# The ring of weight slots, with each slot a tensor of its own, 32 bytes further apart than a multiple of 2048

## The chip, the cores and the metric

The kernel runs on one core of one Trainium2 chip. The metric is the time of one execution on the device in microseconds (us). Lower is better. Weights, inputs and the output lie in HBM; everything else stays in SBUF and PSUM.

## What is computed

Two transformer-like blocks over 512 tokens of width 1024, one after the other. What matters here is that both are mostly matrix products of a 512-token activation with weights that are read once from HBM. The activations are kept transposed, features on the partitions.

```python
# first block, two layers
h = h + fourier_na_mixer(hn, w_in_ab, rpb, w_out_ab)        # layer 0: 1024 -> 2048, 1024 -> 1024
h = h + short_gated_conv_mixer(hn, w_in_c, conv_c, w_out_c) # layer 1: 1024 -> 3072, 1024 -> 1024
h = h + memory_cross_attention(norm(h), m, wq, wkv, wo)     # both; wkv acts on 256 memory rows
h = h + conv_ffn(norm(h), w_up, conv_w, conv_b, w_down)     # both: 1024 -> 4096, 2048 -> 1024
# second block, one layer
proj = u @ w_in                                             # 1024 -> 9232, cut into 12 parts
h = h + merged(retention(proj), gated_delta(proj)) @ w_o
h = h + (silu(a) * b) @ w_down,  a, b = conv(norm(h) @ w_up)  # 1024 -> 5632, 2816 -> 1024
return rmsnorm(h)
```

All of it is float32 in the reference.

## The kernel before

Every large product is cut into weight units of 256 rows by 512 columns. There are 379 of them (`n_units`), numbered u in the order in which they are used by the list `phases`. A unit passes through one of five slots of a ring (`RING = 5`, slot `u % RING`), and in that slot through four hands:

1. SP's queue loads it into `w_raw` (line 410; two transfers of half the width for the feed-forward "up" products). Before it issues, it waits until TensorE has used the unit that had the slot before: `w_used` at least `u - RING + 1`.
2. ScalarE (ACT) copies `w_raw` to `w_hi` in the rounded type fp32r (line 523, `split`), when the load has landed.
3. GpSimd (POOL) subtracts, `w_lo = w_raw - w_hi` (line 486, `lo`). `w_lo` lies on `w_raw`, byte for byte.
4. TensorE (PE) waits for `lo_done` and makes 24 products per unit (line 929, `products`): for each of four blocks of 128 columns and each of the two 128-row halves, three of them, which are hi by hi, hi by the low part of the activation, and lo by hi. The activation is split into high and low parts in the same way (`XH`, `XL`, or the slots of `HID`). Mostly the weights are the stationary operand (128x128) and 512 tokens stream. In the phases by token, and in the second half of each `kv` phase, the activation is stationary and 512 weight columns stream. `kv` (lines 1070 and 1073) has 256 memory rows: eight units of 24 products with 256 columns, then eight units of 12 products with 512 columns, in each of the two layers.

So there are 363 units of 24 products and 16 of 12, together 8,904 products with a ring operand. The other matmuls (attention, retention, delta rule, statistics) are plain float32 and read tiles that are not in the ring.

ACT, DVE and POOL run their own streams in program order, tied by semaphores. ACT's copies of weight units are put between its other work by `split_to`, up to four units (`LEAD`) ahead of the product that it evacuates.

Where things lie in a partition follows from the order of allocation; each tensor starts on a multiple of 32 bytes. `H`, `XH`, `XL` take 16,384 bytes each and start at 1,152. The ring follows: `w_raw` with `w_lo` on it (5 x 4,096 bytes) at 50,304, and `w_hi` (5 x 4,096) at 70,784. So every slot of both, and `XH` and `XL`, start at the same place modulo 2048. Then come `R`, `LNT`, `RC`, `LNC`, `ACC`, `SQ`, `par`, `cst`, `eps_c`, `sm`, and the arena that holds `HID` and all the tiles placed with `at(...)`. Its origin `a0` is pushed up until it equals `w_hi_at` modulo 512; it is 104,064, with 352 bytes skipped, and that is 512 bytes past the ring's place modulo 2048.

Of the kernel before, what the change touches and what calls it, by code (L numbers as in the profile page):

```python
# [18 lines left out]
F32 = mybir.dt.float32  # L19
F32R = mybir.dt.float32r  # L20
# [4 lines left out]
P = 128  # L25
# [6 lines left out]
UC = 512  # L32
# [54 lines left out]
def program(nc, ins, out):  # L87
    ctx = ExitStack()
    with ctx:
        def sb(name, shape, dt=F32):  # L90
            return ctx.enter_context(nc.sbuf_tensor(name, shape, dt))
# [5 lines left out]
        H = sb("H", [P, KT, T])  # L97
        XH = sb("XH", [P, KT, T], F32R)
        XL = sb("XL", [P, KT, T], F32R)
        w_raw = sb("w_raw", [P, RING, 2, UC])  # L100
        w_lo = nc.alloc_sbuf_tensor_at("w_lo", [P, RING, 2, UC], F32R, offset=nc.sbuf_base - RING * 2 * UC * 4)
        w_hi_at = nc.sbuf_base
        w_hi = sb("w_hi", [P, RING, 2, UC], F32R)
        R = sb("R", [P, T])
        LNT = sb("LNT", [P, T])
        RC = sb("RC", [P, NCH])
# [294 lines left out]
        @block.sync  # L401
        def _(sp):
            def load(mat, k, c_of, slot, freed):

                for s, v in freed:
                    sp.wait_ge(s, v)
                view = mat.rearrange("(k p) n -> p k n", p=P)
                at_col = 0
                for c, width in c_of:
                    sp.dma_start(w_raw[:, slot, :, at_col:at_col + width],  # L410
                                 view[:, 2 * k:2 * k + 2, c:c + width]
                                 ).then_inc(w_loaded[slot], 16)
                    at_col += width

            xv = ins["xT"].rearrange("(k p) t -> p k t", p=P)
            sp.dma_start(par[:, :], ins["params"]).then_inc(c_loaded, 16)
            for name, mat, nk, groups in phases:
                u0, per = first[name], nk // 2
                if name == "rqk":
                    sp.wait_ge(h_upd, KT * (rp_index["wo1"] + 1))  # L420
                    for tab, src in ((COS, "rot_cos"), (SIN, "rot_sin"), (AGE, "age")):
                        sp.dma_start(tab[:, :], ins[src]).then_inc(t_loaded, 16)
                if name == "dab":

                    u = u0
                    sp.wait_ge(w_used, u - RING + 1)
                    view = mat.rearrange("(k p) n -> p k n", p=P)
                    dst = w_raw[:, u % RING, :, :].rearrange("p a (b c) -> p (a b) c", c=P)
                    at_col = 0
                    for c, width in groups[0]:  # L430
                        sp.dma_start(dst[:, :, at_col:at_col + width], view[:, :, c:c + width]
                                     ).then_inc(w_loaded[u % RING], 16)
                        at_col += width
                    sp.wait_ge(rg_dve, 6)
                    sp.dma_start(LVM[:, :, :], ins["levels"]).then_inc(l_loaded, 16)
                    continue
                if name == "rv":

                    sp.wait_ge(bn_dve, 4 + KT)
                    sp.dma_start(h_dram, H[:, :, :].rearrange("p k t -> p (k t)")).then_inc(h_saved, 16)  # L440
                for g in range(len(groups)):
                    if name == "wo2" and g == 1:
                        sp.wait_ge(dn_dve, 4)
                        sp.wait_ge(h_saved, 16)
                        sp.dma_start(H[:, :, :].rearrange("p k t -> p (k t)"), h_dram).then_inc(h_back, 16)
                    for k in range(per):
                        u = u0 + g * per + k
                        freed = [(w_used, u - RING + 1)] if u >= RING else []
                        load(mat, k, groups[g], u % RING, freed)
                        if name == "out0" and (g, k) == (0, per - 1):  # L450

                            sp.wait_ge(f1_done, NA_H)
                            mv = ins["memT"].rearrange("(k p) t -> p k t", p=P)
                            sp.dma_start(M[:, :, :], mv).then_inc(m_loaded, 16)
                        if u < KT // 2:

                            sp.dma_start(H[:, 2 * u:2 * u + 2, :], xv[:, 2 * u:2 * u + 2, :]).then_inc(x_loaded[u], 16)
                        if u == 0:
                            sp.dma_start(cst[:, :, :], ins["consts"]).then_inc(c_loaded, 16)
                    if name == "in0" and g == 1:  # L460

                        sp.dma_start(FC[:, :, :], ins["fourier_seq"]).then_inc(f_loaded, 16)
                        sp.dma_start(GC[:, :], ins["fourier_grp"]).then_inc(f_loaded, 16)
                        rp = ins["rpb"]
                        for h in range(NA_H):
                            for i in range(2):
                                src = bass.AP(rp.tensor, (h * 15 + i) * RPB_PW, [[1, GRID_W], [RPB_PW, NA_ROWS], [1, GRID_W]])
                                sp.dma_start(B2[GRID_W * i:GRID_W * (i + 1), h, :, :], src).then_inc(b_loaded, 16)

            ov = out.rearrange("(k p) t -> p k t", p=P)  # L470
            for k in range(KT):
                sp.wait_ge(fin_dve, k + 1)
                sp.dma_start(ov[:, k, :], H[:, k, :]).then_inc(out_stored, 16)
            sp.wait_ge(out_stored, 16 * KT)


        @block.gpsimd
        def _(pool):
            nc.gpsimd.memset(eps_c[:, 0:1], EPS)
            nc.gpsimd.memset(eps_c[:, 1:2], GN_EPS).then_inc(pad_zero, 1)  # L480

            def lo(u):

                s = u % RING
                pool.wait_ge(hi_done, u + 1)
                nc.gpsimd.tensor_tensor(w_lo[:, s, :, :], w_raw[:, s, :, :], w_hi[:, s, :, :].bitcast(F32),  # L486
                                        ALU.subtract).then_inc(lo_done, 1)

            early = first["out0"]
            for u in range(early):  # L490
                lo(u)

            pool.wait_ge(b_loaded, 16 * 2 * NA_H)
            n = 0
            for i in range(2):
                half = B2[GRID_W * i:GRID_W * (i + 1), :, :, :].rearrange("p h s c -> p (h s) c")
                lowc = half[:, :, 0:GRID_W - NA_KW]
                nc.gpsimd.affine_select(out=lowc, in_=lowc, compare_op=ALU.is_ge, fill=-1e30,
                                        base=NA_KW // 2 - (GRID_W - 1),
                                        pattern=[[0, NA_H * NA_ROWS], [1, GRID_W - NA_KW]],  # L500
                                        channel_multiplier=1).then_inc(b2_sel, 1)
                n += 1
                pool.wait_ge(b2_sel, n)
                high = half[:, :, NA_KW:GRID_W]
                nc.gpsimd.affine_select(out=high, in_=high, compare_op=ALU.is_ge, fill=-1e30,
                                        base=NA_KW // 2 - 1 - NA_KW + GRID_W - 1,
                                        pattern=[[0, NA_H * NA_ROWS], [-1, GRID_W - NA_KW]],
                                        channel_multiplier=-1).then_inc(b2_sel, 1)
                n += 1
                pool.wait_ge(b2_sel, n)  # L510
            for u in range(early, n_units):
                lo(u)
# [3 lines left out]
        def _(act):  # L516
            state = {"split": 0}

            def split(u):

                s = u % RING
                act.wait_ge(w_loaded[s], load_value[u])
                nc.scalar.activation(w_hi[:, s, :, :], w_raw[:, s, :, :], ACT.Copy).then_inc(hi_done, 1)  # L523

            def split_to(end):

# [387 lines left out]
        def _(pe):  # L914
            def products(u, k, bank, x_hi_t, x_lo_t, tokens_out, start, stop):
# [3 lines left out]
                for m in range(4):  # L919
                    for j in range(2):  # L920
                        kt = 2 * k + j
                        for n in range(3):
                            wt = w_lo[:, slot, j, :] if n == 2 else w_hi[:, slot, j, :]
                            xt = x_lo_t[:, kt, :] if n == 1 else x_hi_t[:, kt, :]
                            if tokens_out:
                                a, b = xt[:, m * P:(m + 1) * P], wt
# [120 lines left out]
            def kv(l):  # L1047
# [4 lines left out]
                for g in range(4):  # L1052
# [5 lines left out]
                    for k in range(4):  # L1058
# [3 lines left out]
                        for m in range(4 if g < 2 else 2):  # L1062
                            for j in range(2):
                                kt = 2 * k + j
                                for n in range(3):
                                    wt = w_lo[:, s, j, :] if n == 2 else w_hi[:, s, j, :]
                                    xt = ML[:, kt, :] if n == 1 else MH[:, kt, :]
                                    begin, end = kt == 0 and n == 0, kt == KT - 1 and n == 2
                                    if g < 2:
# [291 lines left out]
            def block2():  # L1361
# [12 lines left out]
                u = first["dab"]  # L1374
                pe.wait_ge(lo_done, u + 1)
                pe.wait_ge(rb_dve, 1)
                hi = w_hi[:, u % RING, :, :].rearrange("p a (b c) -> p (a b) c", c=P)
                lo = w_lo[:, u % RING, :, :].rearrange("p a (b c) -> p (a b) c", c=P)
                for kt in range(KT):
                    for n, (a, b) in enumerate(((hi, XH), (hi, XL), (lo, XH))):  # L1380
                        mm = nc.tensor.matmul(ps[:, 0, :], a[:, kt, :], b[:, kt, :], start=kt == 0 and n == 0,
# [715 lines left out]
```

## Time and profile before

| what | value |
|---|---|
| median of 3 runs | 2449.18 us (2447.05 to 2452.76) |
| the profiled execution's own time | 2449.59 us |
| its span, first to last instruction | 2447.8 us |
| PE busy | 2354.3 us, 96% |
| PE weight loads busy | 1922.7 us, 79% |
| DVE, ACT, POOL busy | 999.8, 864.0, 972.0 us |
| DMA | 218.23 MB, mean 89 GB/s |
| granted TensorE clock, mean | 0.990 of 2.4 GHz |

The span leaves out 1.8 us of the execution's own time. A busy PE is not a PE at its peak: the pace of the products is read from how many fit into a stretch without a gap.

### The profile page before, as it was taken

To read this page: it belongs to the slowest core of one execution; us is meant where nothing else is said; L and a number is where in the kernel's file an instruction comes from. 1 tells how busy PE (TensorE), PEld (TensorE's weight loads), DVE (VectorE), ACT (ScalarE), POOL (GpSimd) and SP (SyncE) were. 2 spreads that over 40 slices of the span, in tenths; PEclk is the share of its full clock that TensorE was granted. 3 is DMA by queue.
4 is the path that set the end of the run, shared out by engine and by line. 5 is a ranking of instruction groups with operands and counts; after the bars stand their busy time and mean duration, and the time that the engine had idled before them with its cause. 6 is when DMAs were issued, how large, how long until landed. Compare 5 with 4: busy or idle time off the path is not lost.

```text
span 2447.8 us, 25636 instructions
## 1 busy us (share of the span) xinstructions
PE 2354.3 (96%) x10910; PEld 1922.7 (79%) x10910; DVE 999.8 (41%) x1222; ACT 864.0 (35%) x1044; POOL 972.0 (40%) x389
## 2 busy tenths in 40 slices
PE   8989999999999999999999999988998999999997
PEld 6748878888887887888887668867877888888885
DVE  4253034342143212444237231567368333666601
ACT  4245344233322433432344462351352243322221
POOL 4506524544444642444435224330140144455441
PEclk9999999999999999999999999999999999999998
DMA  6204313333333531333333213420230033333331
GB/s 186 95 17 140 118 44 95 101 98 95 95 95 94 154 96 53 97 101 95 108 111 108 65 44 106 112 65 18 55 84 18 27 95 129 96 102 95 95 96 68
DMA packets 148562, 218.23 MB, mean 89 GB/s; under 512 B 18641, under 2 KB 75217, under 8 KB 148193
## 3 DMA queue, kind: packets, MB, share of 16 engines
q1 hardware_dynamic: 147328, 212.38, 28.9%
q10 hardware_dynamic: 1120, 4.23, 0.5%
q8 instruction: 86, 1.41, 0.2%
q14 instruction: 28, 0.22, 0.0%
HBM read 212.34 MB, written 4.23 MB: 88 GB/s over the span
## 4 chain that ended last, share of the span: by engine, by line
PE 91%; DVE 5%; ACT 2%; issue 1%; DMA 0%; POOL 0%; SPq 0%; DVEq 0%; ACTq 0%
PE ps L929 76%; PE ps L1070 2%; PE ps L1073 2%; PE ps L1291 1%; PE ps L1086 1%; PE ps L1109 1%; DVE MT L1858 1%; PE ps L1280 1%; PE ps L1179 1%; PE ps L1192 1%; PE ps L1016 1%; PE ps L1232 1%; DVE MM L1862 0%; PE ps L952 0%; PE ps L1308 0%
## 5 line engine op out<-in xcount | busy, mean ns | idle before, releaser
L486 POOL TENSOR_TENSOR w_lo<-w_raw,w_hi 128x1024 fp32r<-128x1024 f32 x379 | 960.4, 2545 | 1435.6 <-ACT w_hi L523 1435.4
L929 PE MATMUL ps<-XH,w_hi 128*128 128x512 f32 x1792 | 703.2, 392 | 12.7 <-DVE XL L1419 11.8
L523 ACT ACTIVATE w_hi<-w_raw 128x1024 fp32r<-128x1024 f32 x379 | 395.4, 1056 | 874.0 <-DMA w_raw<-ffn_w_up 123.9
L929 PE MATMUL ps<-XH,w_lo 128*128 128x512 f32 x1792 | 698.3, 390 | 0.0
L929 PE MATMUL ps<-XL,w_hi 128*128 128x512 f32 x1792 | 698.1, 390 | 0.0
L929 PE MATMUL ps<-HID,w_hi 128*128 128x512 f32 x1760 | 542.9, 390 | 4.1 <-DVE TY L1641 2.4
L929 PEld LDWEIGHTS ps<-XH,w_hi 128*128 128x128 f32 x1792 | 337.0, 188 | 85.5 <-issue 14.2
L929 PEld LDWEIGHTS ps<-XL,w_hi 128*128 128x128 f32 x1792 | 337.1, 188 | 71.7 <-issue 2.4
L929 PEld LDWEIGHTS ps<-XH,w_lo 128*128 128x128 f32 x1792 | 336.9, 188 | 70.6
L929 PEld LDWEIGHTS ps<-HID,w_hi 128*128 128x128 f32 x1760 | 330.1, 188 | 74.9 <-issue 3.4
L929 PE MATMUL ps<-HID,w_lo 128*128 128x512 f32 x880 | 342.4, 389 | 0.0
L929 PEld LDWEIGHTS ps<-HID,w_lo 128*128 128x128 f32 x880 | 165.2, 188 | 34.5
L1429 DVE TENSOR_TENSOR H<-ps,H 128x512 f32<-128x512 f32 x64 | 42.3, 683 | 365.0 <-PE ps L929 365.0
L1578 DVE TENSOR_TENSOR GP<-ps,R 128x1024 f32<-128x1024 f32 x16 | 19.6, 1224 | 177.5 <-PE ps L929 177.5
L1280 PE MATMUL ps<-MM,AT 128*128 128x128 f32 x384 | 58.9, 302 | 26.5 <-DVE MM L1862 12.0
L1280 PEld LDWEIGHTS ps<-MM,AT 128*128 128x128 f32 x384 | 50.7, 207 | 34.2 <-DVE MM L1862 18.1
L1529 DVE TENSOR_TENSOR QX<-ps,R 128x2048 f32<-128x2048 f32 x4 | 9.2, 2292 | 157.6 <-PE ps L929 157.6
L1916 DVE SCALAR_TENSOR_TENSOR CV<-GP,par,CV 128x512 f32<-128x512 f32 x88 | 69.9, 863 | 0.0
L533 ACT ACTIVATE SQ<-H 128x512 f32<-128x512 f32 x63 | 39.7, 630 | 64.9 <-DVE H L1429 33.0
L1908 DVE TENSOR_TENSOR GP<-ps,R 128x2048 f32<-128x2048 f32 x11 | 25.2, 2291 | 76.2 <-PE ps L929 76.2
L1291 PE MATMUL ps<-MT,T 128*128 128x128 f32 x384 | 54.9, 285 | 0.5
L1405 DVE TENSOR_TENSOR ACC<-ACC,SQ 128x512 f32<-128x512 f32 x63 | 50.2, 797 | 6.5 <-ACT SQ L533 4.5
(318 smaller groups left out, 2307.0 us busy)
## 6 DMA issues: line engine op xcount, KB each, us to landing
w_raw<-w_in SPq DMA_DIRECT2D x72, 512.0 KB, 3.7
w_raw<-ffn_w_up SPq DMA_DIRECT2D x128, 256.0 KB, 2.9
w_raw<-w_up SPq DMA_DIRECT2D x88, 256.0 KB, 3.1
w_raw<-xa_wkv SPq DMA_DIRECT2D x32, 512.0 KB, 3.6
w_raw<-ffn_w_down SPq DMA_DIRECT2D x32, 512.0 KB, 3.7
w_raw<-w_in_c SPq DMA_DIRECT2D x24, 512.0 KB, 3.7
w_raw<-w_down SPq DMA_DIRECT2D x22, 512.0 KB, 3.6
w_raw<-w_in_ab SPq DMA_DIRECT2D x16, 512.0 KB, 4.1
```

The costliest lines, as they stand in the source:

```text
L486: nc.gpsimd.tensor_tensor(w_lo[:, s, :, :], w_raw[:, s, :, :], w_hi[:, s, :, :].bitcast(F32), ALU.subtract).then_inc(lo_done, 1)
L523: nc.scalar.activation(w_hi[:, s, :, :], w_raw[:, s, :, :], ACT.Copy).then_inc(hi_done, 1)
L533: nc.scalar.activation(ACC[:, :] if c == 0 else SQ[:, :], H[:, c, :], ACT.Square).then_inc(sq_done, 1)
L929: mm = nc.tensor.matmul(ps[:, bank + m, :], a, b, start=start and j == 0 and n == 0, stop=stop and j == 1 and n == 2)
L1070: mm = nc.tensor.matmul(ps[:, bank + m, 0:NMEM], wt[:, m * P:(m + 1) * P], xt, start=begin, stop=end)
L1073: mm = nc.tensor.matmul(ps[:, bank + m, :], xt[:, m * P:(m + 1) * P], wt, start=begin, stop=end)
L1280: mm = nc.tensor.matmul(ps[:, pb(p) + 2, cols_], AT[:, p, cols_], MM[:, p, cols_], start=True, stop=True)
L1291: mm = nc.tensor.matmul(ps[:, pb(p) + 3, cols_], T1[:, p, cols_], MT[:, hh, cols_], start=True, stop=True)
L1405: nc.vector.tensor_tensor(ACC[:, :], ACC[:, :], SQ[:, :], ALU.add).then_inc(acc_done, 1)
L1429: nc.vector.tensor_tensor(H[:, c, :], ps[:, (c + flip) % 8, :], H[:, c, :], ALU.add).then_inc(h_upd, 1)
L1908: nc.vector.tensor_tensor(GP4[:, :, 2:T + 2], banks(bank), over(R[:, :], 4), ALU.mult).then_inc(up2_dve, 1)
L1916: nc.vector.scalar_tensor_tensor(out=CV4[:, q, :], in0=GP4[:, q, i:T + i], scalar=of(w0 + 2 * nf * i, q), in1=CV4[:, q, :], op0=ALU.mult, ...
```

## The change

The three ring tensors become lists of five tensors each. Slot i now holds its `w_raw`/`w_lo` (4,096 bytes), directly behind it its `w_hi` (4,096 bytes), and behind that an unused tensor `gap` of 32 bytes. All uses index the list in place of the slot dimension; shapes, instructions, order and waits stay as they are.

```diff
-        w_raw = sb("w_raw", [P, RING, 2, UC])
-        w_lo = nc.alloc_sbuf_tensor_at("w_lo", [P, RING, 2, UC], F32R, offset=nc.sbuf_base - RING * 2 * UC * 4)
         w_hi_at = nc.sbuf_base
-        w_hi = sb("w_hi", [P, RING, 2, UC], F32R)
+        w_raw, w_lo, w_hi, gap = [], [], [], []
+        for i in range(RING):
+            w_raw.append(sb(f"w_raw{i}", [P, 2, UC]))
+            w_lo.append(nc.alloc_sbuf_tensor_at(f"w_lo{i}", [P, 2, UC], F32R, offset=nc.sbuf_base - 2 * UC * 4))
+            w_hi.append(sb(f"w_hi{i}", [P, 2, UC], F32R))
+            gap.append(sb(f"gap{i}", [P, 8]))
...
-                    sp.dma_start(w_raw[:, slot, :, at_col:at_col + width],
+                    sp.dma_start(w_raw[slot][:, :, at_col:at_col + width],
...
-                nc.gpsimd.tensor_tensor(w_lo[:, s, :, :], w_raw[:, s, :, :], w_hi[:, s, :, :].bitcast(F32),
+                nc.gpsimd.tensor_tensor(w_lo[s][:, :, :], w_raw[s][:, :, :], w_hi[s][:, :, :].bitcast(F32),
                                         ALU.subtract).then_inc(lo_done, 1)
...
-                nc.scalar.activation(w_hi[:, s, :, :], w_raw[:, s, :, :], ACT.Copy).then_inc(hi_done, 1)
+                nc.scalar.activation(w_hi[s][:, :, :], w_raw[s][:, :, :], ACT.Copy).then_inc(hi_done, 1)
...
-                            wt = w_lo[:, slot, j, :] if n == 2 else w_hi[:, slot, j, :]
+                            wt = w_lo[slot][:, j, :] if n == 2 else w_hi[slot][:, j, :]
```

The same replacement stands in the load of the `dab` unit (line 428), in `kv` (line 1066) and in the products of `dab` (lines 1377 and 1378).

## Rows read from the trace of the kernel before

**Rows 1.** The page's busy times of the engines.
```profile
span 2447.8 us, 25636 instructions
PE 2354.3 (96%) x10910; PEld 1922.7 (79%) x10910; DVE 999.8 (41%) x1222; ACT 864.0 (35%) x1044; POOL 972.0 (40%) x389
```

**Rows 2.** The page's chain that ended last, by engine.
```profile
PE 91%; DVE 5%; ACT 2%; issue 1%; DMA 0%; POOL 0%; SPq 0%; DVEq 0%; ACTq 0%
```

**Rows 3.** The chain in order of time: start us, us, what.
```profile
10.87 0.67 DVE XL L1419
11.55 0.25 issue
11.79 19.24 PE ps L929 x72
31.04 0.86 PE ps L952 x2
...
211.54 23.03 PE ps L1070 x192
234.57 21.79 PE ps L1073 x96
...
300.76 6.91 PE ps L1086 x32
...
394.70 261.14 PE ps L929 x1152
...
656.71 114.27 PE ps L929 x504
```

**Rows 4.** Windows: stretch, PE, PEld, DVE, ACT, POOL busy, clock, DMA share, GB/s.
```profile
211.50:234.60 23.10, 23.10 (x194) 23.10 (x193) 7.96 (x12) 13.09 (x16) 16.46 (x8) 1.00 0.61 181
234.60:256.40 21.80, 21.80 (x97) 18.02 (x96) 0.00 (x0) 10.31 (x10) 19.38 (x9) 1.00 0.64 190
400.00:650.00 250.00, 250.00 (x1104) 207.02 (x1103) 94.81 (x105) 78.55 (x88) 120.73 (x48) 1.00 0.32 97
```

**Rows 5.** One line's instructions: ns min/median/max, first and last start.
```profile
L486 POOL TENSOR_TENSOR w_lo<-w_raw,w_hi x379: 2342/2401/6995, 6.9 to 2406.1; 128x1024 fp32r<-128x1024 f32 x190
L523 ACT ACTIVATE w_hi<-w_raw x379: 1039/1060/1065, 5.8 to 2405.0; 128x1024 fp32r<-128x1024 f32 x190
L1587 DVE SCALAR_TENSOR_TENSOR CV<-GP,par,CV x64: 734/739/745, 405.9 to 1162.5; 128x512 f32<-128x512 f32 x64
```

**Rows 6.** DMA issues of the page: KB each, median us to landing.
```profile
w_raw<-w_in SPq DMA_DIRECT2D x72, 512.0 KB, 3.7
w_raw<-ffn_w_up SPq DMA_DIRECT2D x128, 256.0 KB, 2.9
```

**Rows 7.** Timeline of kv of the first layer, POOL and PEld.
```profile
219.98 18.98 POOL L486 TENSOR_TENSOR w_lo<-w_raw,w_hi 128x1024 fp32r<-128x1024 f32 x8 [6.64 <-ACT w_hi L523]
...
222.77 0.19 PEld L1070 LDWEIGHTS ps<-MH,w_hi 128*128 128x128 f32 x1
```

**Rows 8.** The chain after rotary: start us, us, what.
```profile
1312.79 1.07 ACT w_hi L523
1313.86 0.07 issue
1313.93 2.37 POOL w_lo L486
```

**Rows 9.** Who waited for whom: us in total, times, longest.
```profile
POOL w_lo L486 <- ACT w_hi L523: 1435.4, 285, 110.8
SPq L410 <- PE ps L929: 2054.0, 335, 116.6
```

More of the change, by code:

```diff
@@ L427, in _ @@
                     view = mat.rearrange("(k p) n -> p k n", p=P)
-                    dst = w_raw[:, u % RING, :, :].rearrange("p a (b c) -> p (a b) c", c=P)
+                    dst = w_raw[u % RING][:, :, :].rearrange("p a (b c) -> p (a b) c", c=P)
                     at_col = 0
@@ L1065, in kv @@
                                 for n in range(3):
-                                    wt = w_lo[:, s, j, :] if n == 2 else w_hi[:, s, j, :]
+                                    wt = w_lo[s][:, j, :] if n == 2 else w_hi[s][:, j, :]
                                     xt = ML[:, kt, :] if n == 1 else MH[:, kt, :]
@@ L1376, in block2 @@
                 pe.wait_ge(rb_dve, 1)
-                hi = w_hi[:, u % RING, :, :].rearrange("p a (b c) -> p (a b) c", c=P)
-                lo = w_lo[:, u % RING, :, :].rearrange("p a (b c) -> p (a b) c", c=P)
+                hi = w_hi[u % RING][:, :, :].rearrange("p a (b c) -> p (a b) c", c=P)
+                lo = w_lo[u % RING][:, :, :].rearrange("p a (b c) -> p (a b) c", c=P)
                 for kt in range(KT):
```

## The prediction, on record before the changed kernel was run

> **What bounds the kernel.** I read the page's busy times first, then the chain that ended last, then that chain piece by piece, and last the instructions that touch the ring. TensorE is busy 96% of the span [rows 1] and holds 91% of the chain; DMA and POOL have 0% of it [rows 2]. So two questions decide: does the pace of a product change, and does anything that feeds the ring become late?
>
> The pace stands in the pieces of the chain, which have no gap in them [rows 3]. 1,152 products in 261.14 us are 226.7 ns each, and 504 in 114.27 us are 226.7 ns. The first piece holds 768 products on `XH`/`XL` and 384 on `HID` (up0 and down0), the second has `XH`/`XL` alone. The 192 of `kv` with 256 columns take 120.0 ns each, the 96 in which the weights stream 227.0 ns. The granted clock is 1.00 throughout, that is 2.4 GHz [rows 4], so 512 columns at one a cycle are 213.3 ns and 256 are 106.7 ns. A product pays 13.3 ns above its columns, the same for both lengths. A float32 matmul pays much less: 32 with 256 columns take 6.91 us, 215.9 ns each, which is two cycles a column and 2.6 ns.
>
> **The addresses.** After the change slot i starts 32 x i bytes past slot 0, modulo 2048. Inside a slot `w_raw`, `w_lo` and `w_hi` still agree modulo 2048, 4,096 bytes apart where it was 20,480. Slot 0 still agrees with `XH`, `XL`; slots 1 to 4 are 32, 64, 96 and 128 bytes off. Those slots serve 303 of 379 units, some 7,120 of the 8,904 products (four fifths). Behind the ring, `R` to `sm` move up by 160 bytes. The arena doesn't move: its skipped bytes shrink from 352 to 192, and `a0` stays 104,064.
>
> **The cost of each part.**
>
> Instructions, waits, order, queues: none is added, removed or moved. The gap tensors are not accessed. 0 us, nothing hides it because nothing is there.
>
> PE's pace. The trace holds two relations between the addresses of a product's operands: equal modulo 2048 (`XH` with the ring) and 512 apart (`HID` with the ring). Both give 226.7 ns, whichever slot is read, since the mean of a piece of 48 units would show one slow slot in five. The blocks m and halves j step by 512 and 2,048 bytes and leave no mark either. For float32, two matmuls of the statistics read `ACC` (192 past a multiple of 512) against `ones` (256 past one), and take 0.86 us for two, 430 ns each [rows 3]: two cycles a column is 426.7 ns, so a misfit of 64 bytes costs them at most 3.3 ns, about the floor of the others. What no row shows is an fp32r product whose operands differ by something other than a multiple of 512. Its bounds, from the nearest rows: at best the 13.3 ns falls to float32's 2.6 ns, 10.7 ns x 7,120 = 76 us gained; at worst as much is paid once more, 76 us lost. I take 0, since the row nearest in kind, the misfit pair of the statistics, shows none and the surcharge has been the same for every relation so far. But PE decides everything here: 0.7 ns per displaced product is already 5 us.
>
> [...]
>
> POOL and ACT. A subtraction takes 2.40 us and a copy 1.06 us [rows 5]. All three operands of the subtraction shift together, so their mutual distance modulo 4096 stays. Whether POOL minds a start 32 bytes into a 64-byte stretch (slots 1 and 3) no row tells; DVE doesn't mind starts 0, 4 and 8 bytes in, as its three taps on `GP` take 734 to 745 ns [rows 5]. I take 0 for POOL, with bounds of -0.06 (its own minimum, 2.34) and, as a guess at a doubled access, +2.4 us. What hides a slower POOL: PE uses a unit in 24 x 226.7 ns = 5.44 us, and a freed slot is wanted again 4 units = 21.8 us later, while load 3.7 [rows 6], copy and subtraction make 7.2 us. 14.6 us are spare; POOL waits 1435.4 us for ACT in all and SP 2054.0 us for PE [rows 9]. The cover is thin in three places. In each `kv` a unit lasts 2.88 or 2.72 us, and in the first one ACT comes late: POOL begins a run of eight back to back at 219.98, ends the first at 222.39, and PE's loads of that unit begin at 222.77 [rows 7], 0.38 us spare. After the rotary PE waits for one subtraction outright [rows 8]. At +10% (0.24 us) only this last one costs, 0.2 us. At 3.0 us a subtraction, the eight units of 2.72 lose 0.28 each and the eight of 2.88 lose 0.12, about 3 us less 0.4 per layer, some 5.5 us in all; that is the point from which POOL decides. The copies of ACT precede it and the same holds.
>
> DMA. SP issues each load as soon as its slot is free, and it lands 14 us before its use; a load half as long again (+1.9 us) is hidden too. In `kv` the DMA engines are busy 0.64 of the time [rows 4] and the run through slots takes 4 units x 2.72 = 10.9 us against 7.2. At the start PE waits for `XL`, made from `H` [rows 3], which stays where it is. 0 us.
>
> `R` to `sm` moved by 160 bytes. DVE, ACT and the statistics read them. DVE's taps above show no cost of a shifted start. 0 us.
>
> **Sum.** Against the profiled execution: 2449.6 us (span 2447.8 and 1.8 around it) + 0 + 0 + 0 + 0 = 2449.6, and that execution lay 0.4 us above the median of the runs. I predict 2449 us.
>
> **The rivals.**
>
> Same (the sum): 2449, within 2444 to 2454. For it: one pace for every relation in the trace; no feeder on the chain. Chance 0.63.
>
> Slower, at PE: an fp32r product needs a steadier supply of operands than a float32 one, one element a cycle in place of one in two, while the next weights are being loaded. If its two reads meet badly once their starts no longer agree modulo 512, each displaced product pays. For it: the surcharge of 13.3 ns exists for fp32r alone, and every present start is equal modulo 512, so the trace can't clear it. Against: 512 apart and equal are the same to 0.1 ns. Price: 10.7 ns on all four displaced slots is 2525 us; on slots 1 and 3 alone (3,560 products) 38 us, 2487. It decides from 0.7 ns. If only the streaming operand minded, 480 products, four fifths of them x 10.7 = 4 us, and it would hide in the noise. Chance 0.20.
>
> Slower, at POOL: from 3.0 us a subtraction, 2455; at 4.8, both `kv` stages go at POOL's pace: 16 x 4.8 - 44.8 = 32 us each, less a little, and the rotary 2.4: 2510. Chance 0.05.
>
> Faster, at PE: the 13.3 ns is a collision of reads whose starts agree, and goes where they don't: 2449 - 76 = 2373, or 2411 if half of it goes. For it: float32's 2.6 ns. Against: `HID`, 512 apart, pays the same, and float32's `KX` by `QX`, both in the arena and equal modulo 1024, pays 2.6, so agreement alone costs nothing. Chance 0.12.
>
> **Numbers.** Within 0.2% (4.9 us, about what measurements of this kernel can tell from no change): 0.63. Slower: 0.20 + 0.05 = 0.25. Faster 0.12. The range takes the same case whole and reaches up to half of the PE rival and to most of POOL's, 2440 to 2500; outside are the full PE loss (0.07), the far end of POOL's (0.01) and nearly all of the gain (0.11), 0.19. The likeliest case by itself has 2444 to 2454.
>
> **What would show it.** Right: the long pieces of the chain keep 226.7 ns, L1070 keeps 120.0; POOL's median stays 2.40 us and ACT's 1.06 in every slot; the chain keeps PE at 91%. Wrong at PE: the piece of 1,152 products departs from 261.14 us, and starts between products differ by slot, slot 0 alone keeping 226.7. Wrong at POOL: a median above 3 us and waits of PE for `w_lo` in `kv`. What would make me wrong is any effect of a start not a multiple of 512 away, of which the trace has no fp32r example.

## The result, and the profile after

The changed kernel takes 2494.09 us (median of 4 runs, 2492.55 to 2494.46), the kernel before 2448.39: a ratio of 1.0179, 95% interval 1.0164 to 1.0194, 1.8% or 45.7 us slower. I had predicted 2449 and no difference.

The page's head and its chain, to be held against [rows 1, 2]:

```profile
span 2492.2 us, 25636 instructions
...
PE 2397.2 (96%) x10910; PEld 1921.9 (77%) x10910; DVE 992.2 (40%) x1222; ACT 864.5 (35%) x1044; POOL 968.6 (39%) x389
...
PE 92%; DVE 5%; ACT 1%; issue 1%; DMA 0%; POOL 0%; SPq 0%; DVEq 0%; ACTq 0%
```

The span grew by 44.4 us and PE's busy time by 42.9, with the same number of instructions. The other engines worked no longer than before. So it is not a wait for a feeder: TensorE does the same matmuls more slowly. The pieces of the chain without a gap (start us, us, what), against [rows 3]:

```profile
214.18 22.75 PE ps L1073 x192
236.94 22.32 PE ps L1076 x96
...
304.61 6.91 PE ps L1089 x32
...
400.00 267.60 PE ps L932 x1152
668.46 117.09 PE ps L932 x504
```

1,152 products went from 226.7 to 232.3 ns each, the 96 of `kv` with streaming weights from 227.0 to 232.5. The 192 with 256 columns got faster, from 120.0 to 118.5 ns, and the float32 matmuls (L1089, L1086 before) stayed at 6.91 us.

POOL and ACT on the ring, and DVE's taps, min/median/max, against [rows 5]:

```profile
L489 POOL TENSOR_TENSOR w_lo<-w_raw,w_hi x379: 2344/2405/6999, 7.0 to 2449.8; 128x1024 fp32r<-128x1024 f32 x190
...
L526 ACT ACTIVATE w_hi<-w_raw x379: 1035/1060/1066, 5.9 to 2448.7; 128x1024 fp32r<-128x1024 f32 x190
...
L1590 DVE SCALAR_TENSOR_TENSOR CV<-GP,par,CV x64: 733/742/749, 411.2 to 1184.4; 128x512 f32<-128x512 f32 x64
```

All within 0.6% of before. What grew is how long the feeders wait:

```profile
POOL w_lo L489 <- ACT w_hi L526: 1482.5, 284, 112.1
...
SPq L413 <- PE ps L932: 2097.6, 335, 116.7
```

1435.4 became 1482.5 us and 2054.0 became 2097.6 [rows 9]. Both feeders are idle for longer because PE gives the slots back later.

Which products are slow shows in the timeline of one piece. First and last of 22 products of a unit in slot 4, then first and last of 21 of the next unit, in slot 0 (start us, us, engine, line):

```profile
400.30 0.39 PE L932 MATMUL ps<-XH,w_lo 128*128 128x512 f32 x1
...
405.18 0.40 PE L932 MATMUL ps<-XH,w_lo 128*128 128x512 f32 x1
...
405.87 0.39 PE L932 MATMUL ps<-XH,w_lo 128*128 128x512 f32 x1
...
410.40 0.39 PE L932 MATMUL ps<-XL,w_hi 128*128 128x512 f32 x1
```

4.88 us over 21 products is 232.4 ns; 4.53 over 20 is 226.5. The slot decides. The duration column (0.39, 0.40 us) hides it: it is longer than the 0.23 us from one start to the next, so the matmuls overlap; the distance from start to start is the pace. The table has the mean pace by slot from the starts in the two traces: the distance from a product to the next one of the same unit, without `kv` and without intervals of 300 ns or more, in which PE waited (some 1,600 intervals a slot):

```
ns per product        slot 0   slot 1   slot 2   slot 3   slot 4
start past XH, bytes       0       32       64       96      128   (modulo 256, after)
before                 226.8    226.7    226.7    226.8    226.8
after                  228.1    233.1    233.3    233.9    233.3
```

Added up over the starts: the products outside `kv` take 45.8 us more, those of `kv` with 256 columns 0.7 less, those with 512 columns 1.0 more, and the waits and the stretches between the streams 1.9 less. That is 44.2 us between the first and the last ring product (2416.3 before, 2460.5 after), which leaves 0.2 us of the 44.4 to anything else.

### The profile page after: what moved, and what is told of

It is laid out like the page before. It is cut to its first block, busy times and chain, and to the rows that moved or that the text cites. A ratio compares the mean times of both kernels' runs of the same rounds, so it can differ in the third digit from the quotient of the medians.

```text
span 2492.2 us, 25636 instructions
## 1 busy us (share of the span) xinstructions
PE 2397.2 (96%) x10910; PEld 1921.9 (77%) x10910; DVE 992.2 (40%) x1222; ACT 864.5 (35%) x1044; POOL 968.6 (39%) x389
## 4 chain that ended last, share of the span: by engine, by line
PE 92%; DVE 5%; ACT 1%; issue 1%; DMA 0%; POOL 0%; SPq 0%; DVEq 0%; ACTq 0%
PE ps L932 77%; PE ps L1073 2%; PE ps L1076 2%; PE ps L1294 1%; PE ps L1089 1%; PE ps L1283 1%; PE ps L1112 1%; DVE MT L1861 1%; PE ps L1182 1%; PE ps L1019 1%; PE ps L1195 1%; PE ps L1235 1%; DVE MM L1865 0%; PE ps L955 0%; PE ps L1311 0%
## 5 line engine op out<-in xcount | busy, mean ns | idle before, releaser
L489 POOL TENSOR_TENSOR w_lo<-w_raw,w_hi 128x1024 fp32r<-128x1024 f32 x379 | 957.0, 2536 | 1482.7 <-ACT w_hi L526 1482.5
L932 PE MATMUL ps<-XH,w_hi 128*128 128x512 f32 x1792 | 712.2, 397 | 12.8 <-DVE XL L1422 11.9
L932 PE MATMUL ps<-XL,w_hi 128*128 128x512 f32 x1792 | 707.5, 395 | 0.0
L932 PE MATMUL ps<-XH,w_lo 128*128 128x512 f32 x1792 | 707.3, 395 | 0.0
L932 PE MATMUL ps<-HID,w_hi 128*128 128x512 f32 x1760 | 552.8, 395 | 4.0 <-DVE TY L1644 2.4
L682 ACT ACTIVATE EG<-CV,par 128x512 f32<-128x512 f32 x32 | 22.2, 726 | 86.0 <-DVE CV L1590 86.0
```

Source lines behind the costliest of these rows:

```text
L489: nc.gpsimd.tensor_tensor(w_lo[s][:, :, :], w_raw[s][:, :, :], w_hi[s][:, :, :].bitcast(F32), ALU.subtract).then_inc(lo_done, 1)
L932: mm = nc.tensor.matmul(ps[:, bank + m, :], a, b, start=start and j == 0 and n == 0, stop=stop and j == 1 and n == 2)
```

## The experiments

Theory A from here on: the two operands of an fp32r product, the stationary one and the streamed one, clash inside TensorE unless their starts are a certain multiple of bytes apart. Rivals: B, the address of a ring operand by itself counts; C, the new layout, `w_hi` directly behind `w_raw`, makes others' accesses collide with PE's; and smaller ones as they came.

### The layout without the gaps

```diff
             w_hi.append(sb(f"w_hi{i}", [P, 2, UC], F32R))
-            gap.append(sb(f"gap{i}", [P, 8]))
```

> The changed kernel without its gaps: five tensors each, w_hi directly behind w_raw of the same slot, every slot again at one place modulo 2048. Theory A (the two operands of a product clash inside TensorE by how far apart their starts are, modulo 512): 2448 us, 226.7 ns a product in every slot. Rival C (the interleaved layout, with ScalarE, GpSimd and the loads now writing next to what TensorE reads): still about 2494 us and 233 ns. Part-way (both share): 2460 to 2485.

2448.48 us; ratio to before 1.0001 (0.9991 to 1.0011). Every slot at 226.7 to 226.8 ns. Its longest piece:

```profile
394.44 261.14 PE ps L931 x1152
```

261.14 us, to the hundredth what it was [rows 3]. Separate tensors and the interleaving cost nothing; rival C is out. The gaps are the whole change.

### The ring 64 bytes up against XH

```diff
+        pad = sb("pad", [P, 16])
         w_raw = sb("w_raw", [P, RING, 2, UC])
```

> The kernel before with 64 bytes of padding ahead of the ring. XH and XL stay, the ring and, by its own rule, the arena (HID, MH, ML) move up by 64 bytes modulo 512. Theory A (distance between the operands' starts): the 5,688 products on XH and XL go to about 233 ns, those on HID stay at 226.7: 5,688 x 6.5 ns = 37 us, 2485 us. Rival B (where an operand starts by itself): HID's go to 233 as well, 8,900 x 6.5 = 55 us or more, 2500 us. Rival D (only starts that differ from slot to slot cost anything): 2448 us.

2482.78 us, ratio 1.0144 (1.0128 to 1.0160). By operand, from the starts: products on `XH` and `XL` 233.2 to 233.3 ns in all five slots, products on `HID`, which moved along with the ring, 226.7 to 226.9. (The 288 products outside `kv` in which the weights stream against a stationary `XH` or `XL` have 230.4 in the mean.) `MH` and `ML` moved along too, and so `kv` has its old pace:

```profile
214.51 23.03 PE ps L1071 x192
237.54 21.79 PE ps L1074 x96
...
399.40 266.27 PE ps L930 x1152
666.53 117.60 PE ps L930 x504
```

768 products on `XH` by 233.2 and 384 on `HID` by 226.7 make 266.1 us for the first long piece, against 266.27; the 504 on `XH` alone have 233.3 ns each. The same weights at the same address are slow against one partner and fast against the other. That is A in so far as a distance between operands decides, and neither B nor the view that slots must differ from each other.

### Everything 64 bytes up

```diff
+        pad = sb("pad", [P, 16])
         H = sb("H", [P, KT, T])
```

> The kernel before with 64 bytes of padding ahead of everything, H, XH and XL included, so that no distance between two tensors changes. Theory A (distance): 2448 us, 226.7 ns. Rival B (absolute start): 2500 us.

2449.00 us, ratio 1.0005 (0.9996 to 1.0015), 226.7 to 226.8 ns in every slot. Absolute addresses don't matter, at least not 64 bytes of them.

### TensorE alone, many distances

The program loads four tiles, rounds them into `WH`, `WL`, `XH` and `XL` with starts at multiples of 2048, and then issues only matmuls, 48 for each case:

```python
for i in range(REP):
    m, j, t = i // 6 % 4, i // 3 % 2, i % 3
    ...  # bfloat16 takes the tiles WB and XB instead
    a = (WL if t == 2 else WH)[:, ws // 4 + m * P:ws // 4 + (m + 1) * P]
    b = (XL if t == 1 else XH)[:, xs // 4:xs // 4 + n]
    ...  # float32 reads the same two tiles as float32
    mm = nc.tensor.matmul(ps[:, m, 0:n], a, b, start=True, stop=True)
```

> Not the network: TensorE alone runs groups of 48 products in the ring's pattern (two with the high weights, one with the low) on loaded inputs, each group with another distance between the stationary and the streamed operand, and the output is one of the results copied. Theory A: fp32r with 512 columns takes 226.7 ns at distances 0, 512 and 1024 and about 233 ns at 32 to 128 with nothing else running on the chip; moving both operands by 32, 64 or 128 leaves 226.7; moving the stationary one alone costs as much as moving the streamed one. Rival B: moving both costs the same 6.5 ns as moving one. Rival C: all 226.7. With 256 columns about 117 ns where distances differ and 120 where they are equal, as in the kv stages. [...] Open: whether some distance gives fewer than 226.7 ns.

Four windows of it, each from the first product of a case to the first of the next, 48 products: the streamed operand 32 bytes on, then 1024, then both operands 64, then the stationary one alone 64 (columns: PE, PEld, ACT, POOL busy, clock, DMA share, GB/s):

```profile
61.38:72.58 11.20, 11.20 (x49) 9.00 (x48) 0.00 (x0) 0.00 (x0) 1.00 0.01 1
217.18:228.06 10.88, 10.88 (x50) 9.01 (x48) 0.00 (x0) 0.00 (x0) 1.00 0.00 0
238.98:249.88 10.90, 10.90 (x50) 9.01 (x48) 0.00 (x0) 0.00 (x0) 1.00 0.01 2
272.00:283.20 11.20, 11.20 (x50) 9.03 (x49) 0.00 (x0) 0.00 (x0) 1.00 0.00 0
```

11.20 / 48 = 233.3 ns, 10.88 / 48 = 226.7. ACT and POOL are at 0.00 and the DMA nearly so, and the clock is 1.00: the cost needs nothing but TensorE. The third window begins with seven intervals of 230.4 ns in the mean, and then has 226.7, although the case ahead (both operands 32 on) agrees as well: so something at the step from one place to the other disturbs the pace for a few products, and what it is I take up at the end. The mean over the last 24 intervals inside each case, by how far the streamed operand starts past the stationary one:

```
fp32r, 512 columns:  0, 256, 512, 1024 bytes              226.7 ns
                     4                                    236.7
                     16                                   231.7
                     8, 32, 48, 96, 128, 192, 224         233.3
                     64, 320                              228.9
                     160                                  234.4
                     384                                  232.3
                     448, 480                             233.3
  both moved by 32, 64 or 128                             226.7
  stationary alone moved by 32, 64 / 128                  233.3 / 232.7
fp32r, 256 columns:  0, 256, 512                          120.0
                     32, 64 / 128                         117.8 / 118.7
float32, 512 columns: 0, 32, 64, 128                      429.2 each of its two instructions
bfloat16, 512 columns: 0, 32, 64, 128                     215.8
```

So the multiple is 256 bytes, and nothing tried is faster than agreement with 512 columns. 64 on the one side and 64 on the other are not the same (228.9 and 233.3). The slots of the changed kernel fit this table: with the weights 32, 64, 96 and 128 bytes on, the streamed operand starts 224, 192, 160 and 128 past them modulo 256, for which the sweep has 233.3, 233.3, 234.4 and 233.3 ns, and the network 233.1, 233.3, 233.9 and 233.3. bfloat16 and float32 don't mind any of the distances tried (215.8 and 429.2 ns at 0, 32, 64 and 128). And float32 turns out to be two matmul instructions in the trace for each one in the program (384 for 192), so 858 ns for 512 columns. A cycle, here as in the prediction, is what one more column costs an aligned fp32r product: 226.7 - 120.0 = 106.7 ns for 256 columns at a granted clock of 1.00, 2.4 columns a ns. So float32 takes four cycles a column, where I had read two.

### 256 bytes in the network

```diff
-            gap.append(sb(f"gap{i}", [P, 8]))
+            if i == 0:
+                gap.append(sb(f"gap{i}", [P, 64]))
```

> The changed kernel with one gap of 256 bytes behind slot 0 and no other, so that slots 1 to 4 start 256 bytes off XH and XL modulo 512. Theory A as the sweep sharpened it (the distance counts modulo 256): 2448 us, 226.7 ns everywhere. Rival (what counts is a distance modulo 512, and the sweep's 256 is a coincidence of its own addresses), or any separation of the slots other than a multiple of 512: 6.5 ns on some 7,120 products, 2494 us.

2449.19 us, ratio 0.9998 (0.9989 to 1.0008), 226.7 to 226.8 ns in each slot. A gap eight times as wide costs nothing, which fits the multiple of 256.

### One slot in five

```diff
-            gap.append(sb(f"gap{i}", [P, 8]))
+            if i == 3:
+                gap.append(sb(f"gap{i}", [P, 8]))
```

> The changed kernel with one gap of 32 bytes ahead of slot 4 and no other: one slot in five is off by 32 bytes. If each product pays by its own operands: 1,800 products of slot 4 by 6.5 ns, 11.7 us, 2460 us, slot 0 at 226.7. If a product that follows a displaced one pays too until the reads fall back in step, as slot 0 does in the changed kernel (228.05 ns mean): 1,824 x 1.4 = 2.6 us more, 2463 us. Rival (it takes several different starts at once): 2448 us.

2460.05 us, ratio 1.0048 (1.0031 to 1.0065), 11.1 us. Slots 0 to 4: 227.0, 226.7, 226.7, 226.8, 233.1 ns. The dose holds: one slot costs a quarter of what four cost, and slot 0 behind it pays 0.3 ns, not the 1.3 of the changed kernel.

### Other distances, and fewer stationary columns

As the first sweep, with the starts of the four tiles set one by one, and `c` stationary columns:

```python
...
a = w[0][:, w[1] // 4 + m * P:w[1] // 4 + m * P + c]
b = x[0][:, x[1] // 4:x[1] // 4 + n]
```

> Not the network: TensorE alone in groups of 48 products with other distances, only one of the operands displaced, fewer stationary columns and other streamed lengths. If the 10.9 ns that fp32r pays above bfloat16's 215.8 ns is a collision of the read of the stationary operand with the stream, it shrinks with the stationary columns: 64 columns about 221 ns and 32 about 218.5 with aligned starts, and the displaced surcharge shrinks as well. If it is a fixed cost of an fp32r product, 226.7 stays for 64 and 32 columns. Small steps (12, 20, 24, 28, 40, 72, 80, and 4, 8 and 16 back) between 228 and 237 ns; if one is below 226.7 there is something to gain. The low tiles alone displaced: between 226.7 and 233.3, as one or two products in three are hit. Shorter streams: the columns at 2.4 GHz and 13.3 ns more, displaced 6.5 ns more from 384 up and nothing, or less, at 256.

```
512 streamed, 128 stationary columns, both streamed tiles past the weights by
  28, 508 bytes            226.7 ns        12 bytes                    228.9
  248                      230.0           80                          231.1
  24, 40, 504              233.3           20, 72                      236.2, 235.5
  496                      236.7
only XL past by 32 / 64 / 128              233.3 / 231.9 / 233.3
only WL past by 32 / 64 / 128              233.3 / 231.1 / 231.1
WL and XL past by 64 / 128                 231.1 / 231.1
stationary columns 96 / 64 / 32, aligned   230.0 / 230.0 / 231.7;  32 bytes off  233.3 / 230.8 / 233.3
streamed columns 448 / 384 / 320 / 128     206.7 / 173.3 / 146.7 / 111.7;  32 bytes off  204.4 / 173.3 / 146.7 / 111.7
```

Here the expectations failed in part. The 10.9 ns that aligned fp32r pays above bfloat16 does not shrink with the stationary columns; it grows. So it isn't a collision whose size follows the weights read. One low tile out of line, which concerns one product in three, costs the pattern in the mean the full 6.7 ns at 32 bytes, and 4.4 to 6.7 at 64 and 128, not a third of it. And a misfit of 32 bytes costs 6.7 ns with 512 columns only: it is nil at 128, 320 and 384, and a gain of 2.2 ns at 256 and 448, where I had expected a loss from 384 up. Nothing is below 226.7 ns at 512 columns, so the network has nothing to gain from another distance there.

### One gap of 32 bytes, all four slots at the same place

```diff
-            gap.append(sb(f"gap{i}", [P, 8]))
+            if i == 0:
+                gap.append(sb(f"gap{i}", [P, 8]))
```

> The changed kernel with one gap of 32 bytes behind slot 0 and no other: slots 1 to 4 all start 32 bytes off XH and XL. Theory A (every distance counts for itself; the sweep gave 233.3 ns at 32): 2494 us as in the changed kernel, 233.3 ns in slots 1 to 4 and about 228 in slot 0. Rival (five different starts are what costs): nearer to 2460, as with one odd slot.

2492.39 us, ratio 1.0175 (1.0157 to 1.0193); 227.1 ns in slot 0, 233.1 to 233.4 in the others. The variety of starts is not what costs.

### Only the small tiles moved

```diff
         w_hi = sb("w_hi", [P, RING, 2, UC], F32R)
+        pad = sb("pad", [P, 40])
```

> The kernel before with 160 bytes of padding behind the ring, so that only R, LNT, RC, LNC, ACC, SQ, par, cst, eps_c and sm move, as far as the change moves them. Theory A: 2448 us, no product that reads the ring is touched. Rival (part of the 44 us comes from these tiles, read by DVE, ScalarE and the statistics): above 2453 us.

2448.69 us, ratio 0.9998 (0.9988 to 1.0008). `R` to `sm` are free to move.

### Another slot made the one that agrees

```diff
         w_hi_at = nc.sbuf_base
+        pad = sb("pad", [P, 48])
```

> The changed kernel with the whole ring 192 bytes further up, and the arena where it was: modulo 256 it is now slot 2 that starts where XH, XL and HID start, while slots 0, 1, 3 and 4 are 192, 224, 32 and 64 past it. Theory A modulo 256, with the sweep's paces: slot 2 has 227 to 228.5 ns as slot 0 had, slots 1, 3 and 4 about 233, slot 0 between 229 and 233; 2485 to 2494 us. Rival (slot 0 or the first tensor is special, or the 256 bytes do not carry over): no slot below 231, or slot 0 the fast one.

2484.39 us, ratio 1.0144 (1.0127 to 1.0160). Slots 0 to 4: 229.6, 233.3, 226.8, 233.1, 233.2 ns. First and last of 20 products of a unit in slot 1, then of 14 of the next one in slot 2:

```profile
409.95 0.40 PE L933 MATMUL ps<-XH,w_hi 128*128 128x512 f32 x1
...
414.39 0.39 PE L933 MATMUL ps<-XL,w_hi 128*128 128x512 f32 x1
...
416.93 0.39 PE L933 MATMUL ps<-XH,w_hi 128*128 128x512 f32 x1
...
419.87 0.39 PE L933 MATMUL ps<-XL,w_hi 128*128 128x512 f32 x1
```

4.44 us over 19 is 233.7 ns, 2.94 over 13 is 226.2; with the starts to the nanosecond it is 233.3 and 226.7. The fast slot is now slot 2. Slot 0, whose weights start 192 past `XH`, so that `XH` is 64 past them modulo 256, has the sweep's odd value for 64 (228.9 there, 229.6 here).

No kernel here beats the one before. The gain at 256 columns is 384 products by 2.2 ns, 0.8 us, and the same tiles would then be out of line in the 192 products of `kv` with 512 columns, 1.0 us as measured above; I didn't run that.

## Why the prediction was wrong

**PE's pace: the step that failed.** I took 0, "since the row nearest in kind, the misfit pair of the statistics, shows none and the surcharge has been the same for every relation so far". Both halves were weak. The pair is float32 (one product of the program, in two instructions), and the sweep shows that float32 doesn't mind any distance tried, 32, 64 and 128 (429.2 ns an instruction at each), where fp32r does (233.3, 228.9 and 233.3 against 226.7); it was near in size of misfit and far in kind of product. And "every relation so far" were two, equal and 512 apart, which are one and the same modulo 256. I saw that the trace could not clear the displaced case and said so, and still gave it 0.20. What the runs put in place of the 0: 6.7 ns a product on slots 1 to 4 (the mean of the four) and 1.3 on slot 0, 45.8 us outside `kv`. The sign that I had named for it came: 261.14 us became 267.60, and the starts differ by slot.

**The rival of a loss at PE was the right one.** That two reads meet badly is my guess, shown by no run; that a displaced fp32r product pays is shown. Its price was too high: 10.7 ns, worked out as the difference of two surcharges, against 6.7 measured. Nothing in the runs ties the cost to that difference: float32 is two instructions of two cycles a column each (429.2 ns for 512 columns), so its 2.6 ns is the surcharge of half a product, and the second sweep shows that the fp32r surcharge doesn't follow the size of the weights read (226.7 ns with 128 stationary columns, 230.0 with 64). Its sub-case, slots 1 and 3 only, is wrong: all four pay. Its condition, "no longer agree modulo 512", should read 256. That a product with streaming weights pays like the others was right: 227.0 to 232.5 ns.

**The rival of a gain** came true in the one place I didn't price, the 256-column products of `kv`, 0.7 us in all. That a misfit is cheaper there is shown (117.8 ns at 32 bytes against 120.0 in the sweep); why is not.

**The other engines** have no part in the cost: the displaced pace is the same with TensorE alone (233.3 ns at 32 bytes) and in the network (233.1).

**POOL, ACT, DMA and the small tiles** were right at 0: 2.405 us a subtraction, 1.060 a copy, no wait of PE that was not there before, and 2448.69 us with the small tiles moved alone. The row that I read for three taps of DVE holds two of them, 4 and 8 bytes in; the tap at 0 is another instruction (L1582, 561 ns in the median). Nothing hung on it. The range of 2440 to 2500 held the 2494, on the strength of the rival.

**What stays open.** Why 256 bytes, and by what in TensorE a start out of line costs time. With agreement the paces at 512, 448, 384, 320 and 256 columns (226.7, 206.7, 173.3, 146.7, 120.0 ns) are all multiples of 6.67 ns, which is 16 columns at 2.4 a ns, and the usual price of a misfit with 512 columns is one such step. That suggests a regular turn that a product has to wait for, but no run shows it; and 111.7 ns at 128 columns, the 230.0 of fewer stationary columns, 28 and 508 bytes, which cost nothing, and 64 with its two sides don't follow from it. Those two distances were measured on TensorE alone, not in the network.

Nor is it shown between which two operands the distance counts. I have spoken of the two operands of one product, but in the trace the weights are loaded during the product ahead. From the kernel before (start us, us, engine, line):

```profile
400.00 0.39 PE L929 MATMUL ps<-XH,w_hi 128*128 128x512 f32 x1
400.00 0.19 PEld L929 LDWEIGHTS ps<-XL,w_hi 128*128 128x128 f32 x1
400.23 0.39 PE L929 MATMUL ps<-XL,w_hi 128*128 128x512 f32 x1
```

The load at 400.00 is for the product at 400.23, and it runs while the product at 400.00 streams. In the sweeps the loads stand in the same order. So it may be the stream of one product and the weights of the next whose distance counts. Inside a unit of the network both readings give the same distances, so its runs can't tell them apart. Two cases of the sweeps can in part, and neither reading explains both. Between two cases that both agree (1024 bytes, then both operands 32 on) only the next weights lie 32 bytes off a stream, once, and the pace is disturbed for seven intervals. With both low tiles moved together by 64 or 128 every stream meets next weights that agree, while two products in three have operands that don't, and the pattern has 231.1 ns, not 226.7. What is shown is that agreement of all the tiles is fast and that starts out of line cost; which pair pays stays open. The advice below holds either way.

## What to carry to other kernels

In a stream of fp32r matmuls with 512 columns, let all stationary and streamed operands, the low parts too, start at the same place modulo 256 bytes; it was worth 1.8% here, and a padding of 32 bytes between them undoes it. Look for it in the distance from start to start, not in the duration of a matmul, and compare by buffer. Before taking a cost as 0 because it never changed in a trace, count how many different cases of it the trace really holds.

## What I had not expected of the hardware

- Addresses inside a partition change TensorE's pace: 226.7 ns with agreement modulo 256 bytes, up to 236.7 at 4 bytes off, and 233.3 at most distances, for fp32r; nothing for bfloat16 (215.8) and float32 (429.2 an instruction).
- At 256 columns, and at 448, the sign turns: 120.0 against 117.8 ns, 206.7 against 204.4.
- The pace has a memory. An aligned slot behind a displaced one needs some products to fall back: in slot 0 of the changed kernel the first eight intervals of a unit have 230.6 ns in the mean and the others 226.6 to 227.1, which makes 228.1.
- A displaced stream is not even. In slot 1 of the changed kernel intervals of 232.0 and 234.7 ns alternate.
- Fewer stationary columns make an aligned product slower, not faster: 230.0 ns with 96 or 64, 231.7 with 32.
